# Dilated heads of a hybrid encoder: the keys' rests multiplied as two half-high matmuls side by side

## What is computed

```python
def banded_attention(q, k, v, half):      # called for (window, dilation) in (128, 1), (512, 4), (2048, 16)
    ...
    sc = jnp.einsum('bnqhd,bnkhd->bnhqk', qp, kw, preferred_element_type=jnp.float32) * (d ** -0.5)
    sc = jnp.where(mask[None, :, None], sc, NEG_INF)
    m = jnp.max(sc, axis=-1, keepdims=True)
    p = jnp.exp(sc - m)
    den = jnp.sum(p, axis=-1)
...
outs, lses -> w = softmax(lses); o = sum(outs * w)
```

## Time and profile before

| | |
|---|---|
| median of 3 runs | 2857.73 us (2855.75 to 2864.28) |
| the profiled execution | 2857.64 us, its span 2855.8 us |
| TensorE busy | 2796.6 us, 98%, 14256 matmuls |
| VectorE busy | 1685.2 us, 59% |
| ScalarE busy | 1058.7 us, 37% |
| granted TensorE clock, mean of the core | 0.995 of full speed |
| dilated heads run | from 472 us in layer 0 and to 2021 us in layer 1, by the bias pass |

### The profile page before, as it was taken

The page is one execution under the profiler, slowest core; times in us unless marked ns, Lnnn a source line. Parts: engine busy times, 40 slices in busy tenths (PEclk is TensorE's granted clock), DMA queues, the critical chain, the costliest instruction groups (busy, mean ns, idle before and its releaser), DMA issues.

```text
span 2855.8 us, 38973 instructions
## 1 busy us (share of the span) xinstructions
PE 2796.6 (98%) x14256; PEld 2390.3 (84%) x14256; DVE 1685.2 (59%) x2890; ACT 1058.7 (37%) x1954; POOL 229.6 (8%) x375
## 2 busy tenths in 40 slices
PE   8999999999999999999999999999999999999998
PEld 7998888878888888888798988888788888888887
DVE  6642888875545555455566438888745555455455
ACT  5332888883211111111244238888722111111112
POOL 0000452100000000000100013411000000000000
PEclk9999999999999999999999999999999999999999
DMA  5656884312111111111146577744211111111111
GB/s 200 195 186 205 191 200 114 90 68 81 45 44 44 54 49 44 44 58 52 46 177 189 173 219 189 183 101 97 74 67 45 55 48 44 44 58 45 44 51 59
DMA packets 150322, 283.57 MB, mean 99 GB/s; under 512 B 15024, under 2 KB 104752, under 8 KB 140464
## 3 DMA queue, kind: packets, MB, share of 16 engines
q1 hardware_dynamic: 139568, 252.45, 29.2%
q0 software_dynamic: 10624, 29.41, 3.7%
HBM read 208.90 MB, written 72.88 MB: 99 GB/s over the span
## 4 chain that ended last, share of the span: by engine, by line
PE 90%; DVE 4%; issue 3%; ACT 1%; DMA 1%; DVEq 0%; SPq 0%; ACTq 0%
PE ps L1540 24%; PE ps L1356 22%; PE ps L1555 19%; PE ps L1436 8%; PE ps L1450 7%; PE ps L1482 6%; PE ps L1316 1%; PE ps L1475 1%; PE ps L1492 1%; PE ps L1398 1%; PE ps L1427 1%; DVE x L1270 1%; DVE vbuf L1257 1%; ACT rbuf L932 1%; DVE hn L1011 1%
## 5 line engine op out<-in xcount | busy, mean ns | idle before, releaser
L1555 PE MATMUL ps<-w_dn,hid 128*128 128x512 f32 x3072 | 711.8, 391 | 1.4
L1540 PE MATMUL ps<-hT,w_up 128*128 128x512 f32 x3072 | 702.5, 389 | 3.3 <-DVE hT L994 3.3
L1555 PEld LDWEIGHTS ps<-w_dn,hid 128*128 128x128 f32 x3072 | 574.0, 188 | 132.4 <-DVE x L1270 14.0
L1540 PEld LDWEIGHTS ps<-hT,w_up 128*128 128x128 f32 x3072 | 576.2, 188 | 123.1 <-ACT rbuf L932 3.8
L1356 PE MATMUL ps<-ws,hT 128*128 128x384 f32 (+3 forms) x2688 | 520.8, 352 | 6.1 <-DVE hT L994 5.0
L1356 PEld LDWEIGHTS ps<-ws,hT 128*128 128x128 f32 x2688 | 467.2, 192 | 38.1 <-DVE hT L994 5.5
L1270 DVE TENSOR_TENSOR x<-ps,x 128x512 f32<-128x512 f32 x512 | 343.0, 689 | 227.4 <-PE ps L1555 226.2
L1257 DVE TENSOR_TENSOR vbuf<-rbuf 128x512 f32<-128x512 f32 x128 | 88.6, 692 | 370.6 <-ACT rbuf L932 370.6
L994 DVE TENSOR_TENSOR pT<-ps,pT 128x512 fp32r<-128x512 f32 (+1 forms) x448 | 281.6, 664 | 6.8 <-ACT pT L879 5.7
L932 ACT ACTIVATE rbuf<-ps 128x512 f32<-128x512 f32 x128 | 76.6, 598 | 553.9 <-PE ps L1540 553.9
L879 ACT ACTIVATE pT<-ps 128x512 fp32r<-128x512 f32 (+1 forms) x448 | 240.7, 581 | 92.6 <-PE ps L1450 89.6
(11 more groups left out here) (94 smaller groups left out, 2265.1 us busy)
## 6 DMA issues: line engine op xcount, KB each, us to landing
raw<-in_wstream SPq DMA_DIRECT2D x76, 1024.0 KB, 4.8
head<-feats SPq DMA_DIRECT2D x192, 256.0 KB, 6.0
feats<-tst SPq DMA_DIRECT2D x128, 192.0 KB, 2.6
values<-vst POOLq DMA_DIRECT2D x32, 384.0 KB, 3.3
head<-values SPq DMA_DIRECT2D x24, 512.0 KB, 4.0
biasC<-in_bias_c SPq DMA_DIRECT2D x16, 768.0 KB, 11.5
raw<-in_wstream SPq DMA_DIRECT2D x12, 768.0 KB, 5.8
x_park<-x SPq DMA_DIRECT2D x16, 512.0 KB, 8.5
```

Source lines behind the costliest of these rows:

```text
L1540: last = pe.matmul(ps[:, k % 2, :], w_up[slot_of(l, 1 if first else 0)][:, w1, kt, ft * P:(ft + 1) * P], hT[:, w2, kt, sh * 512:(sh + 1) * ...
L1555: last = pe.matmul(ps[:, 2 + m % 4, :], hid[slot_of(l + 1, slot)][:, w1, ft, s * P:(s + 1) * P], w_dn[slot_of(l, 0 if last_group else 1)][ ...
```

## The change

A dilated head gets a seventh feature transfer: the queries' leading words also on partitions 64 to 127, in the free columns 3072 to 4095. An item's two matmuls with the keys' leading words stay as they are, and come first. The two with the keys' rests now contract 64 partitions each: the first half of the keys with the queries' leading words on partitions 0 to 63, the second half with the copy on partitions 64 to 127. The product of the queries' rests with the keys' rests is no longer computed for these heads. A and C heads keep their matmuls in their order. The two waits on `split_lo` are raised by 2, the number that VectorE adds at its start.

```diff
@@ load_features
+                if kind == "B":
+                    sp.dma_start(hb[64:128, 3072:4096], feats[HI, fq:fq + HD, :]).then_inc(head_in[k], 16)
                 if kind == "A":
@@ next_split, on POOL
                 pool.wait_ge(split_hi, l * NU + NU + half + 1)
-                pool.wait_ge(split_lo, l * NU + NU + half)
+                pool.wait_ge(split_lo, l * NU + NU + half + 2)
@@ VectorE, start of a layer
                 if l:
-                    dve.wait_ge(split_lo, l * NU + 2)
+                    dve.wait_ge(split_lo, l * NU + 2 + 2)
                     for hf in range(2):
                         split_job(l, "bq", hf)
@@ scores, on TensorE
                     else:
-                        for kh in range(2):
-                            cols = slice(kh * 512, kh * 512 + 512)
-                            qt = hb[:, q * P:(q + 1) * P]
-                            mm = [(qt, hb[:, 1024 * (1 + w):1024 * (2 + w)][:, cols]) for w in range(2)]
-                            if kind == "A":
-                                mm.append((hb[:, 3072 + q * P:3072 + (q + 1) * P], kR[l % 2][:, cols]))
-                            for k, (a, b) in enumerate(mm):
-                                last = pe.matmul(ps[:, b0 + kh, :], a, b, start=(k == 0), stop=(k == len(mm) - 1))
+                        cols = [slice(kh * 512, kh * 512 + 512) for kh in range(2)]
+                        qt, q3 = hb[:, q * P:(q + 1) * P], hb[:, 3072 + q * P:3072 + (q + 1) * P]
+                        k_hi, k_lo = hb[:, 1024:2048], hb[:, 2048:3072]
+                        if kind == "A":
+                            for kh in range(2):
+                                mm = [(qt, k_hi), (qt, k_lo), (q3, kR[l % 2])]
+                                for k, (a, b) in enumerate(mm):
+                                    last = pe.matmul(ps[:, b0 + kh, :], a, b[:, cols[kh]], start=(k == 0), stop=(k == 2))
+                        else:
+                            for kh in range(2):
+                                pe.matmul(ps[:, b0 + kh, :], qt, k_hi[:, cols[kh]], start=True, stop=False)
+                            for kh, qh in enumerate((qt, q3)):
+                                rows = slice(64 * kh, 64 * kh + 64)
+                                last = pe.matmul(ps[:, b0 + kh, :], qh[rows, :], k_lo[rows, cols[kh]], start=False, stop=True)
                     last.then_inc(s_done, 1)
@@ end of the file
-HEAD_DMAS = {"A": 6 + 4, "B": 6, "C": 6}
+HEAD_DMAS = {"A": 6 + 4, "B": 6 + 1, "C": 6}
```

## The result

The changed kernel takes 2871.52 us (median of 5 runs, 2869.4 to 2873.9) against 2857.73 us before: a ratio of 1.005, with an interval of 1.0039 to 1.0062. (The kernel before was run five times beside it, 2855.75 to 2864.28, with the same median as its first three.) It is slower by 13.8 us, half a per cent, more than the 0.3% that can be told from no change. The forecast, 2838 us with a range of 2835 to 2867, was wrong in sign, and the result lies in the range of rival (c), 2866 to 2887 us.

What follows compares the result with a forecast made beforehand. The prediction took TensorE to bound the dilated heads: 2857.64 us, less 22.1 for side-by-side half-high products, plus 2.4 for ScalarE and VectorE, transfer and waits 0, gives 2838 us, range 2835 to 2867.

Steps and rivals of the forecast that it cites:

- rival (c): Score products of dilated heads: array empties at each change of height, 159 to 266 ns each, 2866 to 2887 us; chance 0.27.
- What bounds the kernel: Dilated heads: TensorE has no idle time in a head of 22.62 us, and VectorE and ScalarE wait for it.
- The pair runs side by side: Dilated items' two half-high score products: start together and cost one product, saving 0.230 us an item, 22.1 us.
- (a): Half-high pair: second load issued late, second product starts 107 ns late, only 11.8 us saved, 2846 us; chance 0.17.
- (b): Half-high pair: products go one after another at 0.230 us each, or a small stop, 2857.6 us; chance 0.14.
- I take the best value: Scores of dilated items: both loads hidden under the preceding full product, no stop at a height change, 22.1 us saved.
- a turn of the sign at 115: Changes into and out of the half-high pair: from 115 ns a change on, the gain becomes a loss.
- the worst case: Scores of dilated items: a height change stops the pipeline, losing 88 to 302 ns an item, 8.4 to 29.0 us.
- the best case: Scores of dilated items: the pair costs one product, 0.230 us saved per item, 22.1 us in all.
- What ScalarE and VectorE give back: Dilated heads: ScalarE's lag costs 0.1 us per block of four items, 2.4 us; bounds 0 and 11 us.
- The transfer and the waits: Seventh feature transfer on SP's queue per dilated head and the two corrected waits: covered by other work, cost 0.

## Why the prediction was wrong

**What bounds the kernel: right.** The dilated heads are TensorE-bound, and each 0.23 us taken from or added to TensorE showed in full: one product less is 0.226 us an item, one pair more 0.232.

**The pair runs side by side: right.** 0.227 us of overlap out of 0.230. The rivals (a), late second load, and (b), one after another, both fall: the two products of a pair last 502 ns and end 0.50 us after their common start, and three pairs follow each other in 0.89 us.

**The step that failed** is the sentence "I take the best value", with its reason that the transposes show loads sustained at 109 ns and "nothing in the trace gives a reason for a stop". It put the price of a change of height at nothing, by the premise that both loads of the pair are done under the full product ahead of it. They are not: they start 0.32 us after it, 0.09 behind its stream, and are exposed, and the same happens again behind the pair. That the loads can be sustained says nothing of a change of height, of which the trace before had not one. The bounds for it held: I had 159 to 266 ns a change, a turn of the sign at 115, and 8.4 to 29.0 us for it, and measured are 182 ns and 13.8 us, of which 12.5 in the dilated heads. The value should have been taken from the worst case, or given the larger chance, since the best case rested only on the absence of rows. The one source that named the matter, the Trainium skill (TensorEngine Tiling (Array Packing), Key Properties), says that changing the tiling mode drains the engine. I gave that rival 0.27. The trace agrees that a change stops the engine, at some 0.18 us; whether it is drained in that time the trace doesn't show. The other rule cited there, that of the Trainium skill (TensorE: Matmul & The Clock Gate, part 3) that matmuls on different row groups start about 4 ns apart, agrees with the trace, where the two of a pair start 3 ns apart. I weighed the two as if one excluded the other. A price for the change and a pair side by side both show here, and the sum needed both.

**The terms within rival (c).** I made the low end of the price from an empty array, 389 - 230 = 159 ns, and the high end with the exposed load added, 266. Measured, the load is exposed (502 against 389 ns), but the stop ahead of it is shorter than 159: 0.201 us a change with full products on both sides, less the load's 107, leaves some 90 ns, as the starts above do. On the way out transposes swallow part of the load. So the measured price lies in my bounds, but neither bound had its parts right: that it lies there is in part luck.

**What ScalarE and VectorE give back:** charged at 2.4 us for the gain. With one product less, where that gain is there, the stretch shows 0.2 us a layer at most. In the changed kernel the question didn't arise: they have more cover than before, not less (VectorE waits 24.3 us a layer for scores there, against 18.1). **The transfer and the waits:** cost 0, as predicted (1.0002).

Open is what TensorE does in the 90 ns: the profile calls it "issue". The loads of the pair start at 503.27, before the last full product's record ends at 503.35, which speaks against a load that waits for an empty array; but the ends of matmuls are modelled, and no run here tells an array that runs empty from another kind of stop.

## What to carry to other kernels

Half-high matmuls side by side do give two products for the time of one, but going in and out of them costs TensorE about 0.18 us each time: one pair of 512 columns saves 0.23 us and two changes cost 0.36, so by these numbers at least two such pairs must stand between the changes to come out ahead. The nearest run to that, two pairs behind one another in every second item, gained 1.1 us a layer where 2.5 were expected. Having all neighbours of the same height would avoid the changes; no run here had that. If the trace of before has no row of an instruction's shape, "nothing in the trace speaks against it" is no evidence: run that instruction between its neighbours alone first, or keep the costly rival inside the range.

## What was not expected

The price is not in the half-high instruction. The same full-high product holds 0.23 us behind one of its own height and 0.43 behind a half-high one, and a transpose group of which nothing was changed grows from 0.87 to 1.02 us. A price of a change has two parts of about the same size, a stop of some 90 ns and an exposed load of 107. Half-high products among themselves are as fast as full ones, even with two weight loads under each pair (six products in 0.89 us).
